# An attention step in another order: thresholds ahead of masked maxima, the next transposed block ahead of exponentials and counts

## The reference, cut to what matters

```python
score = sum_h w[t,h] * relu(q_idx[t,h] . k_idx[s])     # 4 indexer heads, causal
_, sel = lax.top_k(score, 256)                          # the keys that a query keeps
s = (q . k[sel]) * ATTN_SCALE                           # 8 heads, 2 kv heads
pr = softmax(s, axis=-1)
o = pr @ v[sel]
mix = concat([o, pool_out]) @ w_o ; h = x + rmsnorm(mix)
...                                                     # then an MLP, a gate and an embedding
```

## Time and profile before

| | |
|---|---|
| median of 3 runs | 3109.91 us (3106.7 to 3110.88) |
| profiled execution | 3106.33 us, of which its span is 3104.5 us |
| TensorE matmuls busy | 2899.8 us (93%) |
| VectorE busy | 1720.9 us (55%) |
| ScalarE busy | 1384.4 us (45%) |
| mean granted TensorE clock | 0.958 of full speed |

### The profile page before, as it was taken

The page is one execution under the profiler, slowest core; times in us unless marked ns, Lnnn a source line. Parts: engine busy times, 40 slices in busy tenths (PEclk is TensorE's granted clock), DMA queues, the critical chain, the costliest instruction groups (busy, mean ns, idle before and its releaser), DMA issues.

```text
span 3104.5 us, 37743 instructions
## 1 busy us (share of the span) xinstructions
PE 2899.8 (93%) x14264; PEld 2400.8 (77%) x14264; DVE 1720.9 (55%) x3405; ACT 1384.4 (45%) x2235; POOL 390.2 (13%) x447
## 2 busy tenths in 40 slices
PE   8989978788888888999999999999999999999987
PEld 7989855666766767887888888888888888888866
DVE  4476777878988788534333444333543435353343
ACT  4344464857668387555322342233423334332232
POOL 2333412121130400000000010000100001000000
PEclk9999979898899988999999999999999999999998
DMA  4211232211211010123332323323234333233321
GB/s 143 65 53 54 66 108 56 62 51 38 70 38 36 28 34 25 58 79 114 107 129 95 122 95 122 129 95 122 95 115 136 95 101 116 95 122 129 95 95 41
DMA packets 224628, 266.51 MB, mean 86 GB/s; under 512 B 58176, under 2 KB 160320, under 8 KB 224448
## 3 DMA queue, kind: packets, MB, share of 16 engines
q1 hardware_dynamic: 222144, 255.72, 26.1%
q10 hardware_dynamic: 2304, 8.39, 0.7%
HBM read 224.07 MB, written 40.01 MB: 85 GB/s over the span
## 4 chain that ended last, share of the span: by engine, by line
PE 78%; DVE 8%; issue 5%; ACT 5%; POOL 2%; DVEq 0%; ACTq 0%; POOLq 0%
PE bank L1818 58%; PE bank L1973 6%; PE bank L1953 6%; PE bank L1838 2%; PE bank L1939 2%; PE bank L1839 2%; ACT kept L1010 2%; DVE kept L1390 1%; POOL score L910 1%; PE bank L1787 1%; DVE probs L1562 1%; ACT score_tail L1010 1%; ACT probsT L1142 1%; DVE too_few L1398 1%; ACT probs L1113 1%
## 5 line engine op out<-in xcount | busy, mean ns | idle before, releaser
L1597 DVE TENSOR_TENSOR w_lo<-w_raw,w_hi 128x1024 fp32r<-128x1024 f32 x296 | 361.5, 1222 | 558.5 <-ACT w_hi L1124 558.3
L1124 ACT CAST w_hi<-w_raw 128x1024 fp32r<-128x1024 f32 x296 | 308.7, 1044 | 641.2 <-PE bank L1818 639.2
L1953 PEld LDWEIGHTS bank<-values,probsT 128*128 128x128 f32 x2176 | 313.7, 213 | 198.8 <-ACT probsT L1142 141.4
L1953 PE MATMUL bank<-values,probsT 128*128 128x64 f32 x2176 | 322.0, 293 | 121.7 <-ACT probsT L1142 95.8
L1818 PE MATMUL bank<-hn_hi,w_hi 128*128 128x512 f32 x1024 | 405.3, 396 | 0.0
L1818 PE MATMUL bank<-hn_hi,w_lo 128*128 128x512 f32 x1024 | 401.1, 392 | 0.0
L1818 PE MATMUL bank<-w_hi,hid_hi 128*128 128x512 f32 x1024 | 399.0, 390 | 0.0
L1818 PE MATMUL bank<-w_lo,hid_hi 128*128 128x512 f32 x1024 | 398.6, 389 | 0.0
L1818 PE MATMUL bank<-w_hi,hid_lo 128*128 128x512 f32 x1024 | 398.4, 389 | 0.0
L1818 PE MATMUL bank<-hn_lo,w_hi 128*128 128x512 f32 x1024 | 398.2, 389 | 0.0
L1010 ACT ACTIVATE kept<-score,threshold 128x1024 bf16<-128x1024 f32 (+4 forms) x160 | 251.9, 1575 | 96.6 <-DVE threshold L1407 71.1
(11 more groups left out here) (203 smaller groups left out, 4926.1 us busy)
## 6 DMA issues: line engine op xcount, KB each, us to landing
w_raw<-in_w_up SPq DMA_DIRECT2D x64, 1024.0 KB, 5.6
w_raw<-in_w_down SPq DMA_DIRECT2D x64, 1024.0 KB, 5.0
w_raw<-in_w_ple_gate SPq DMA_DIRECT2D x16, 1024.0 KB, 5.0
x_in<-in_x SPq DMA_DIRECT2D x16, 512.0 KB, 3.7
q_t<-q_scratch SPq DMA_DIRECT2D x32, 256.0 KB, 3.7
x_t<-in_x SPq DMA_DIRECT2D x16, 512.0 KB, 4.3
h_scratch<-h_t SPq DMA_DIRECT2D x16, 512.0 KB, 2.9
hnT_scratch<-hn2T_t SPq DMA_DIRECT2D x16, 512.0 KB, 4.2
```

The costliest lines, as they stand in the source:

```text
L1124: nc.scalar.copy(piece_parts(p, w_hi[:, p % 4, :]), raw_piece(p)).then_inc(w_hi_rdy, 1)
L1597: nc.vector.tensor_tensor(piece_parts(p, w_lo[:, p % 4, :]), raw_piece(p), piece_parts(p, w_hi[:, p % 4, :]).bitcast(F32), ALU.subtract).t ...
L1953: last = nc.tensor.matmul(bank[:, 4, h * HEAD:(h + 1) * HEAD], probsT[:, m % 3, a * P:(a + 1) * P], values[:, kt, HEAD * kv:HEAD * (kv + 1 ...
```

## The change

Two orders are changed, no instruction is added or removed. On VectorE `move_pending()` goes ahead of the masks of a step. On ScalarE the copy of the transposed block gets a function, is called once ahead of the loop for step 0, and then in step m for step m+1, ahead of that step's exponentials. Its waits move with it: `pT_ps` for the transposes of step m+1 and `pv_ps` for the product with the values of step m-2, which used the same buffer.

```diff
+            def copy_turned(m):
+                H, b = steps[m]
+                w = blocks[H // Q_HEADS][b][1]
+                act.wait_ge(pT_ps, m + 1)
+                if m >= 3:
+                    act.wait_ge(pv_ps, m - 2)
+                nc.scalar.copy(probsT[:, m % 3, 0:w], bank[:, 1 + m % 3, 0:w]).then_inc(pT_ev, 1)
+
             split_queries(0, 0)
             split_queries(0, 1)
             for H in range(3):
                 exp(H)
+            copy_turned(0)
             for m, (H, b) in enumerate(steps):
                 i, h = divmod(H, Q_HEADS)
-                w = blocks[i][b][1]
-                act.wait_ge(pT_ps, m + 1)
-                if m >= 3:
-                    act.wait_ge(pv_ps, m - 2)
-                nc.scalar.copy(probsT[:, m % 3, 0:w], bank[:, 1 + m % 3, 0:w]).then_inc(pT_ev, 1)
+                if m + 1 < len(steps):
+                    copy_turned(m + 1)
                 for next_H in exp_at[m]:
                     exp(next_H)
...
                 if b == 0 and h == 0 and i >= 1:
                     outputs(i - 1)
+                move_pending()
                 for next_H, c in score_at[m]:
                     mask_block(next_H, c)
-                move_pending()
```

## The result

| | before | changed |
|---|---|---|
| median of 4 runs | 3108.3 us | 3080.64 us (3078.5 to 3086.31) |
| span of the profiled execution | 3104.5 us | 3077.0 us |

The ratio is 0.9916 (95% interval 0.9903 to 0.9928); a second measurement gave 0.9921 (0.9907 to 0.9934). So 0.8% is gained, 26 us by the ratio and 27.7 us between the two medians, where 38 (to 3070) had been forecast: faster, inside the range, and smaller than said.

The account below looks back on a forecast made before the run. VectorE's list was taken to measure the round stretches, where no engine is full and each waits in turn. Terms -42 + 9 - 4 = -37 us gave 3069.3 from 3106.3, or 3073 by the median; forecast 3070, range 3040 to 3104.

Parts of the forecast that it names:

- Bound and place: In the five round stretches no engine is full; what VectorE idles can be saved; from 1250 us nothing is to be had.
- Copies a step ahead: Round stretches: VectorE's 49.7 us of waits for score products ahead of masks nearly all fall; 42 us saved.
- Copies at the head of ScalarE's queue: ScalarE's list: a copy's new wait for TensorE's transposes is covered by the old one; cost zero.
- Thresholds ahead of masks: VectorE's round: ScalarE's count begins 0.6 to 0.8 us earlier; by itself saves nothing where VectorE is later.
- ScalarE's lateness: Last two round stretches: steps with an exponential make ScalarE late, so VectorE waits at the threshold; +9 us, ends 0 and +49.
- (b): Round stretches: ScalarE takes the wait over, most exponential steps ending late at the threshold; 35 us back, 3096 us, chance 0.14.
- The other stretches: Attention outside the round stretches: half of TensorE's 7.5 us of waits for copies becomes time; -4 us (0 to -8).
- The signs: Changed profile: copy waits under 20 us, mask waits under 12, count waits 20 to 30, last round stretch 10 us shorter.
- (a): Attention: TensorE's clock comes up as waits go, in the round stretches and the five others; 3048 us, chance 0.12.
- (c): Round stretches: slower, as the ring closes in the 54 steps where TensorE is late; 3142 us, chance 0.10.
- the ring: Round's loop: mask behind threshold, behind ScalarE's count, behind copy, behind TensorE's transposes, behind a score bank a mask frees.
- (d): Round stretches: no gain, waits only change names since another edge of the round is as late; 3110 us, chance 0.08.

## Why the prediction was right, and where it was not

**Bound and place: right.** The gain lies in the round stretches (24.3 of 27.5 us of span), the stretch in which TensorE is full did not move, and what VectorE idled was what could be saved.

**Copies a step ahead: right in the main, over-sized by 7 us.** Forecast -42 us of waits ahead of masks, measured -34.6 (49.7 to 15.1), so that more is left than the 12 us of the forecast's upper end. Of the 15.1 us 12.4 lie in the first two round stretches, and they are no waits for a copy. The two longest, 5.0 us together, follow the output projection of the tile before, here the first:

```profile
433.93 7.11 PE L1979 MATMUL bank<-wo_sb,mixT_t 128*128 128x512 f32 x16 [0.84 <-ACT h_t L1091]
...
441.49 0.34 PE L1845 MATMUL bank<-k_parts,q_lo 128*128 128x384 f32 x1
...
441.98 0.56 DVE L1568 CUSTOM_DVE_ANT_0 probs<-bank,mask 128x384 f32<-128x384 f32 x1 [2.60 <-PE bank L1845]
```

TensorE has no idle time in these 7.11 us and the granted clock is 1.00. It is the same ahead of each of the 14 masks that wait over 0.3 us (14.2 of the 15.1 us): TensorE was busy throughout the last 4 us, and 2 to 7 matmuls of the projection lie in them. The same place cost 3.20 us in the kernel before (the mask at 444.64), behind the same 16 matmuls. So the step that failed is that the prediction gave the waits ahead of masks one cause, the late copy, and sized what would be left by 11 to 14 matmuls a step, 2.6 to 3.3 us and at the lower clock only; a projection's matmul has 512 columns and takes over 0.4 us at the higher clock. TensorE's new waits for exponentials (39.8 us, nowhere in the prediction) are not the cause: 23.4 us of them lie in the last three stretches, where 2.7 us of waits ahead of masks are left, and with the exponentials earlier they went from 5.4 us to nothing in the second stretch, while the waits ahead of masks stayed (6.0 and 6.1).

**Copies at the head of ScalarE's queue: right.** In the round stretches ScalarE waits 0.4 us for transposes. The 86.2 us of such waits between 401 and 1192 us cost nothing that the stretches show.

**Thresholds ahead of masks: wrong in its reason.** "By itself that saves nothing where VectorE is the later engine": the sum has no gain for it anywhere, and yet alone it saves 14.9 us; how much of that is the wait filled and how much the earlier count is open, as said above. In the sum it did no harm, because next to the copies it adds 1.3 us, which may be nothing.

**ScalarE's lateness: the other step that failed in size.** Forecast +9 us, measured +16.5 (14.8 to 31.3). The replay took one exponential and two counts and found 0.7 us in the last stretch, 0.3 in the fourth, nothing in the first three. But every stretch grew, by 1.0, 2.4, 2.9, 2.7 and 7.5 us. In the first three the new order on VectorE does it: with the threshold alone moved the wait is the same there (4.3, 6.8 and 5.9 us against 4.2, 6.8 and 5.9), with the copies alone it is less (3.8, 5.0 and 3.1), since a mask fills part of it. In the last two the exponential is late, and it does not come alone. In step 216 it stands with two pieces of a norm, 1.69 + 0.58 + 0.58 us and their reads of the accumulators, some 3 us. Shortening the exponentials removed 11.7 us of the wait, 10.9 of them in the last three stretches; moving them off such steps made the last two stretches shorter, though less by this wait than by the one for the split. The prediction had these lumps under rival (b), and gave (b) 35 us; it came to about half.

**The other stretches**: forecast -4, measured -2.8. **The sum**: -34.6 + 16.5 - 2.8 = -20.9, where the forecast was -37 and the span shows -27.5. Most of the rest is in three waits of VectorE that the prediction gave no term: the queries' split (13.9 to 11.2 us), the last product of a tile ahead of line 1573 (2.7 to nothing) and the pooling's product ahead of line 1322 (1.9 to nothing), less 1.8 us by which VectorE's work is longer. The gaps too small for the list of waits are as before (14.4 and 14.7 us). So both sized terms erred the same way, by 15 us together, and it is luck that some 6 us without a term brought the time nearer to the forecast.

**The signs.** The last round stretch became 11.5 us shorter and the stretch in which TensorE is full stayed as long, as said. Three limits were missed by little: 21.9 us of waits for copies where under 20 was said, 15.1 us ahead of masks where under 12 was said, and 31.3 us for the count where 20 to 30 was said.

**The rivals.** (a) the clock did not come up as a whole: 0.82, 0.84, 0.82, 0.94 and 0.89 in the round stretches against 0.79, 0.85, 0.83, 0.93 and 0.81, and lower in some of the others (0.90 against 0.94). The rule weighed in the prediction, of the Trainium skill's "TensorE: Matmul & The Clock Gate", section "HAM oscillation — how this bites in real kernels", on idle gaps shows in the last stretch at most, 0.89 for 0.81. Even there the time does not hang on it: with the copies alone that stretch had 0.85 and took 127.8 us. No run changes the clock alone. (b) happened in part, beside the forecast and not instead of it. (c) did not: the ring never closed. (d) half did: 16.5 us of 34.6 came back under another name, with 39.8 us of new waits of TensorE that cost little, as the last two placements of the exponentials show. That these waits "have a single cause in the rows", held against (d), was wrong, as said under the copies.

## What to carry to other kernels

Where in-order engines meet once in a step, look for the product that waits for a short copy behind a long instruction, and move the copy; a step's lead was enough here. Then sum each engine's instructions step by step, not over the stretch: two engines with equal sums still wait for each other where one has all its long work in the same step, and moving an exponential to a neighbouring step was worth 10 to 14 us, about half as much as the change itself. Look also at the sizes of an engine's instructions in a step and not at their number: what was left of the waits here stood behind one engine's own long work. And two reorderings that each save time alone may be after the same wait: 21.5 and 14.9 us made 22.8.

## What the runs showed of the hardware that I had not expected

TensorE's granted clock fell to its lower level across short gaps. Between the two pieces of the earlier trace rows it went from 1.00 to 0.50, over a place whose longest waits were 1.30 and 1.41 us (columns as in the earlier trace rows):

```profile
1168.00:1172.00 4.00, 2.70 (x19) 2.05 (x17) 3.90 (x13) 2.91 (x4) 0.00 (x0) 1.00 0.23 66
1172.00:1176.00 4.00, 2.59 (x17) 2.22 (x16) 3.06 (x6) 3.97 (x7) 0.00 (x0) 0.73 0.02 6
```

And removing three quarters of TensorE's waits for copies did not bring it back: in the second round stretch it was 0.85 before and 0.84 after. TensorE's share of idle time hardly fell, since other waits came in the place of these.
